# A streaming-encoder block in split float32: value groups' outputs moved to the end of a step, a projection's wait narrowed to its own bank, its pieces spread over other steps

## What is computed

```python
h = rmsnorm(x)
a_q, a_k, a_v, b_q, b_k, b_v, c_q, c_k, c_v, c_f, gates = split(h @ w_in)
# A: 4 heads, two score maps each, mask by chunks, value width 128
a = softmax(q1 @ k1.T * scale + bias) - lam * softmax(q2 @ k2.T * scale + bias)
o_a = rmsnorm(a @ a_v) * (1 - lam_init)
# B: 8 heads of 64, a band of at most 5 key tiles of 128 a query tile
o_b = softmax(b_q @ b_k.T * scale + rel_bias, over the band) @ b_v
# C: 8 heads of 64, causal, with a cumulative forget bias
o_c = softmax(c_q @ c_k.T * scale + c_i - c_j, causal) @ c_v
x = x + (sum_i sigmoid(gates_i) * (o_i @ w_br_i)) @ w_out
x = x + (silu(g) * u) @ w_down, with g, u = split(rmsnorm(x) @ w_gate_up)
out = rmsnorm(x)
```

## Time and profile before

| | |
|---|---|
| median of 3 runs | 2151.11 us (2147.57 to 2158.26) |
| the profiled execution | 2156.16 us, span 2154.3 us |
| TensorE busy | 1988.8 us, 92% of the span |
| VectorE busy | 999.7 us, 46% |
| ScalarE busy | 710.8 us, 33% |
| GpSimd busy | 94.5 us, 4% |
| mean granted TensorE clock | 0.98 |

### The profile page before, as it was taken

One profiled execution on the slowest core, in us unless ns is written; L12 is line 12 of the kernel. 1 busy time (PEld: TensorE's weight loads), 2 busy tenths in 40 slices (PEclk: granted clock), 3 DMA queues, 4 the chain that ended last, 5 costly groups with the idle time before them and its releaser, 6 DMA issues. The chain is left out here.

```text
span 2154.3 us, 26265 instructions
## 1 busy us (share of the span) xinstructions
PE 1988.8 (92%) x9542; PEld 1647.9 (76%) x9542; DVE 999.7 (46%) x1950; ACT 710.8 (33%) x1310; POOL 94.5 (4%) x59
## 2 busy tenths in 40 slices
PE   7888988888888888899999999999999999999997
PEld 3777777777777777778787887878888888888886
DVE  4355555565556556732433225754333333333326
ACT  5344444554545445522233112241111111111122
POOL 1110100100100000000000000000000000000000
PEclk9999999999999999999999999999999999999998
DMA  6412222122212211031211113102111111111111
GB/s 218 127 50 50 75 64 61 43 50 61 68 49 50 69 53 31 30 118 44 83 45 53 49 44 147 59 20 59 59 49 31 47 49 58 49 49 29 49 59 78
DMA packets 145268, 133.32 MB, mean 62 GB/s; under 512 B 7476, under 2 KB 130484, under 8 KB 142888
## 3 DMA queue, kind: packets, MB, share of 16 engines
q1 hardware_dynamic: 141768, 132.16, 20.8%
q10 hardware_dynamic: 3424, 0.17, 0.1%
HBM read 109.17 MB, written 16.06 MB: 58 GB/s over the span
## 5 line engine op out<-in xcount | busy, mean ns | idle before, releaser
L182 PE MATMUL ps<-h_hi,w_hi 128*128 128x512 f32 x1664 | 674.3, 405 | 51.2 <-DVE k_stack L745 37.4
L184 PE MATMUL ps<-h_hi,w_lo 128*128 128x512 f32 x1664 | 658.9, 396 | 0.0
L183 PE MATMUL ps<-h_lo,w_hi 128*128 128x512 f32 x1664 | 658.8, 396 | 0.0
L182 PEld LDWEIGHTS ps<-h_hi,w_hi 128*128 128x128 f32 x1664 | 318.8, 192 | 121.9 <-DVE k_stack L745 37.0
L184 PEld LDWEIGHTS ps<-h_hi,w_lo 128*128 128x128 f32 x1664 | 318.7, 192 | 69.5
L183 PEld LDWEIGHTS ps<-h_lo,w_hi 128*128 128x128 f32 x1664 | 319.6, 192 | 62.0
L1598 DVE TENSOR_TENSOR residual<-residual,ps 128x512 f32<-128x512 f32 x240 | 162.6, 685 | 113.9 <-PE ps L184 109.2
L956 PE MATMUL ps<-ident_r,probs_bc 128*128 128x128 f32 x528 | 85.2, 285 | 51.9 <-DVE probs_bc L813 36.3
L1589 DVE TENSOR_TENSOR w_lo<-w_raw,w_hi 128x1024 fp32r<-128x1024 f32 x46 | 56.4, 1226 | 158.4 <-ACT w_hi L1491 158.4
L1499 ACT ACTIVATE bias<-ps 128x512 f32<-128x512 f32 x44 | 26.1, 594 | 311.5 <-PE ps L184 311.5
L184 PE MATMUL ps<-w_down_hi,act_lo 128*128 128x512 f32 x320 | 124.5, 389 | 0.0
(11 more groups left out here) (202 smaller groups left out, 2714.9 us busy)
## 6 DMA issues: line engine op xcount, KB each, us to landing
w_raw<-in_w_in SPq DMA_DIRECT2D x60, 512.0 KB, 3.8
w_raw<-in_w_gate_up SPq DMA_DIRECT2D x44, 512.0 KB, 3.7
k_stack<-k_stack SPq DMA_DIRECT2D x24, 512.0 KB, 6.4
w_raw<-in_w_down SPq DMA_DIRECT2D x22, 512.0 KB, 3.5
x_all<-in_x SPq DMA_DIRECT2D x8, 512.0 KB, 8.7
bias<-bias_a_scratch SPq DMA_DIRECT2D x4, 1024.0 KB, 5.9
heads_bc_scratch<-heads_out SPq DMA_DIRECT2D x8, 512.0 KB, 3.1
bias<-neg_c_scratch SPq DMA_DIRECT2D x4, 1024.0 KB, 5.3
```

Source lines behind the costliest of these rows:

```text
L182: nc.tensor.matmul(out, w_hi, x_hi, start=first, stop=False)
L183: nc.tensor.matmul(out, w_hi, x_lo, start=False, stop=False)
L184: return nc.tensor.matmul(out, w_lo, x_hi, start=False, stop=last)
```

## The change

Four things change, all in attention. The outputs of value groups (`o_low_*` on ScalarE, `o_out_*` on VectorE) move from the start of an odd step to its end. For it the inverse row sums of A get eight columns instead of four, and a value group of B and C waits for the output of the group before it (`c["outs"] + g`), where it waited for the one before that. Groups 1 and 2 of a projection go to banks 6 and 1 (from 1 and 6), and a group waits for the emptying of the last group that used its own bank. The scores of step 8 wait for three emptied groups of the next unit instead of two. The tables of pieces, emptying and slabs change.

```diff
-PIECES_AT = [2, 2, 2, 2, 0, 2, 2, 0, 2, 2, 0, 1, 1, 1, 1, 0, 0]
-EVAC_AT = {0: 0, 2: 1, 4: 2, 7: 3, 10: 4, 16: 5}
-SPLIT_AT = {0: 1, 5: 2, 10: 3}
+PIECES_AT = [2, 2, 2, 2, 1, 1, 1, 1, 0, 1, 1, 1, 1, 1, 1, 2, 0]
+EVAC_AT = {0: 0, 2: 1, 4: 2, 8: 3, 13: 4, 16: 5}
+SPLIT_AT = {0: 1, 4: 2, 8: 3}
+PROJ_BANKS = (3, 6, 1, 6, 6, 6)
...
@@ ScalarE, and in the same way VectorE with o_out_a and o_out_bc
                 for s in range(STEPS + 2):
-                    if b == 0 and s >= 3 and s % 2 == 1:
-                        o_low_a(c, (s - 3) // 2)
-                    if b > 0 and s >= 3 and s % 2 == 1:
-                        o_low_bc(c, (s - 3) // 2)
...
+                    if b == 0 and s >= 3 and s % 2 == 1:
+                        o_low_a(c, (s - 3) // 2)
+                    if b > 0 and s >= 3 and s % 2 == 1:
+                        o_low_bc(c, (s - 3) // 2)
...
@@ TensorE, piece
                 if part == 0 and not (isinstance(unit, int) and unit == 0):
-                    pe.wait_ge(proj_out, 6 * unit + g)
+                    same = [x for x in range(g) if PROJ_BANKS[x] == PROJ_BANKS[g]]
+                    pe.wait_ge(proj_out, 6 * unit + (same[-1] + 1 if same else 0))
@@ TensorE, score
                 if s == STEPS // 2 and not last:
-                    pe.wait_ge(proj_out, 6 * c["unit"] + 8)
+                    pe.wait_ge(proj_out, 6 * c["unit"] + 9)
@@ TensorE, times_v_bc
-                if g >= 2:
-                    pe.wait_ge(o_out, c["outs"] + (g - 1))
-                elif b == 1 and g == 0:
-                    pe.wait_ge(o_out, c["outs"])
+                pe.wait_ge(o_out, c["outs"] + g)
```

More of the change, by code:

```diff
@@ L442, in block_attention @@
         mask_tile = heads[:, 0:P]
-        neg_max, shift, rowsum, rinv = (sb(n, [P, 4]) for n in ("neg_max", "shift", "rowsum", "rinv"))
+        neg_max, shift, rowsum = (sb(n, [P, 4]) for n in ("neg_max", "shift", "rowsum"))
+        rinv = sb("rinv", [P, 8])
         ratio = sb("ratio", [P, 2])
@@ L479, in proj_bank @@
                 return bank(ps, (0, 1, 2, 3, 5, 6)[g] if unit == 0 else 6)
-            return bank(ps, (3, 1, 6, 6, 6, 6)[g])
+            return bank(ps, PROJ_BANKS[g])
         def pv_half(g):
@@ L674, in o_low_a @@
                 nc.scalar.activation(o_low[:, i % 2 * P:(i % 2 + 1) * P], pv_bank[:, P:2 * P], ACT.Copy,
-                                     scale=rinv[:, 2 * (i % 2):2 * (i % 2) + 1]).then_inc(o_low_ready, 1)
+                                     scale=rinv[:, 2 * (i % 4):2 * (i % 4) + 1]).then_inc(o_low_ready, 1)
             def o_low_bc(c, g):
@@ L819, in mix_maps @@
                 dve.wait_ge(probs_ready, c["step"] + (2 * i + 2))
-                nc.vector.reciprocal(rinv[:, q:q + 2], rowsum[:, q:q + 2]).then_inc(rinv_ready, 1)
+                r = 2 * (i % 4)
+                nc.vector.reciprocal(rinv[:, r:r + 2], rowsum[:, q:q + 2]).then_inc(rinv_ready, 1)
                 dve.wait_ge(rinv_ready, c["outs"] + (i + 1))
-                nc.vector.tensor_scalar(ratio[:, i % 2:i % 2 + 1], rowsum[:, q:q + 1], rinv[:, q + 1:q + 2],
+                nc.vector.tensor_scalar(ratio[:, i % 2:i % 2 + 1], rowsum[:, q:q + 1], rinv[:, r + 1:r + 2],
                                         keep["neg_lam"][:, :], ALU.mult, ALU.mult).then_inc(ratio_ready, 1)
@@ L836, in o_out_a @@
                 nc.vector.scalar_tensor_tensor(out=heads[:, i * P:(i + 1) * P], in0=pv_bank[:, 0:P],
-                                               scalar=rinv[:, 2 * (i % 2):2 * (i % 2) + 1], in1=o_low[:, i % 2 * P:(i % 2 + 1) * P],
+                                               scalar=rinv[:, 2 * (i % 4):2 * (i % 4) + 1], in1=o_low[:, i % 2 * P:(i % 2 + 1) * P],
                                                op0=ALU.mult, op1=ALU.add).then_inc(o_out, 1)
@@ L864, in unit_body @@
                 for s in range(STEPS + 2):
[L865 to L868, removed]
                     if b == 0 and s % 2 == 0 and s < STEPS:
@@ L878, in unit_body @@
                         chunks_low(b, c, s)
+                    if b == 0 and s >= 3 and s % 2 == 1:
+                        o_out_a(c, (s - 3) // 2)
+                    if b > 0 and s >= 3 and s % 2 == 1:
+                        o_out_bc(c, (s - 3) // 2)
             for g in range(4):
```

## The result

The changed kernel takes 2069.27 us (median of 4 runs, 2067.87 to 2072.79) where the kernel before, timed beside it, takes 2154.69 (4 runs, 2147.57 to 2161.72). The ratio is 0.961, with a 95% interval of 0.957 to 0.964: 85 us faster. The forecast was 2064 in a range of 2030 to 2112. The profiled execution has 2067.87 us, where the prediction's sum, made against the profiled execution of before, gave 2067.

A forecast was written before the change was run, and what follows sets the result against it. Only attention can gain: TensorE's work plus 106.7 us of waits and 28 us of low clock. Waits 11 + 33 + 26 = 70 us and clock 19 give 89 off, so 2064 us, range 2030 to 2112.

The forecast's parts named there:

- Term 1: Attention's projection pieces wait only for their own bank; the k_stack waits, 37.4 us, go and nothing takes their place.
- Term 2: Pieces in steps 4 to 15 cover softmax-chain waits; B falls from 42.2 us by 33, C from 35.2 by 26.
- turn(9): In B, the turn behind the emptying of group 3 at step 8 waits 1.55 us in place of 2.44.
- Turn(10): In B, the weight slab split at step 8 holds up a scaling and delays this turn by 0.35 us.
- a scaling of 512 columns took 1.20 us ... so 0.65 more: VectorE's scaling at step 8 takes 0.65 us more while GpSimd splits a weight slab.
- the 12 us that the prediction put beside its sum by that page: If scalings stand still for GpSimd's whole 2.40 us instruction, the saving is 12 us less in seven units; not adopted.
- Term 3: Outputs at the step's end: waits for the previous output in A, about 4.5 us a unit; covered in B and C.
- In the same measure: In attention, the clock's cost of 28 us falls like the waits, by two thirds, 19 us.
- The rival by the page TensorE: Matmul & The Clock Gate of the Trainium skill: Clock stays low in attention though waits go; 2081 us, chance 0.15 of the main forecast case (itself 0.70).
- (b): Rival: only k_stack waits go, late softmax-chain waits stay as latency; 2109 us, range 2095 to 2130; chance 0.17.
- (e): Rival: slower, value groups wait for the exponential everywhere; 2177 us at 1.2 us a group; chance 0.04.
- The signs: Right if no k_stack wait, B and C units 9 to 11 us shorter, A 3 to 6, clock 0.98 or more.

The follow-up runs named there:

- The quarters: Changed kernel with GpSimd's low part of a weight slab made in four instructions of a quarter each in attention: 2065.81 us, 0.959 of the kernel before.
- the slab at step 14: Changed kernel with the last weight slab of a unit split in step 14 instead of 8: 2061.26 us, 0.958 of the kernel before.

## Why the prediction was right, and where its terms were off

**What bounds the kernel.** Right. The feed-forward block did not move, and in attention the time is TensorE's work, its waits and the clock: in the sum 60 us of waits and 26 of clock went (27 by TensorE's busy time), 86 of the 88 us between the two profiled executions. The rest is 1.1 us before and behind the eleven units, and rounding.

**Term 1.** Right: 37.4 us of k_stack waits go, and what takes their place is the 1.1 us on w_lo in A, which was not forecast; shown by the banks alone, where the waits of the softmax chain stay to 0.2 us.

**Term 2.** The mechanism was right, the term mis-sized: B keeps 15.9 us, not 9.4, C 16.3, not 9.2. That most late waits want cover, and get it from the spread pieces, is shown by the tables alone (65 to 30 us). In the second unit of B, turn(9) was forecast at 1.55 and measured at 1.80; its chain left out a link, that the turn's bank must be freed by the first low chunk behind the scaling. Turn(10) was forecast at 0.35 and measured at 1.39. In a unit of C, turn(9) has 2.09 for 1.6, turn(10) 0.96 for 0.35, and 1.13 at turn(6), which was not forecast, also behind a scaling held by GpSimd. The held scalings are most of the error: 4 x 1.04 + 3 x (0.61 + 1.13) = 9.4 of the 13.6 us by which B and C kept more. It rests on the step "a scaling of 512 columns took 1.20 us ... so 0.65 more": this is how long the scaling is held when GpSimd began 1.5 us earlier, as in the earlier trace rows, not what the meeting costs. Begun 0.27 us after it, as in the new order, a scaling of 640 columns is held 1.92 us. The earlier trace rows could have told so: the scaling there ends 0.30 us behind GpSimd's instruction. The quarters (no scaling held by more than 0.5 us) and the slab at step 14 both bring B's waits to 10.2 us, 5.7 less. The Trainium skill (SBUF — State Buffer, section "Who interferes with whom") says that the loser stands still for the other's whole instruction; the trace agrees, with 2.47 us against 0.55 where both begin together, and the 12 us that the prediction put beside its sum by that page are near these 9.4.

**Term 3.** The three waits in A are where they were put: in the first unit 0.77 us at step 8 (forecast 1.2), 1.57 at step 10 (2.0), 0.72 at step 13 (1.1), so A keeps 14.4 us instead of 18. B and C have next to no wait on heads_out (0.7 us in all), and in the kernel with the outputs alone, which has no pieces in the late steps, they have 12.4: the cover of piece, score and turn was the right reason. What failed is the view of the move in A as a price alone: against the kernel without it A gains 15 us, 7.7 of waits and 7.0 of clock, because the second score read and the emptying of group 4 come earlier.

**The clock.** Forecast 19 us back, measured 28 less 2, so 26. "In the same measure" as the waits is the step that was off: a third of 28 us should have stayed. By the other experiments there is no such measure: the outputs alone took 4 us of waits and 19 of clock away; with more waiting in A the clock rose to 1.00, with less waiting in B (15.9 to 10.2 us) it fell from 1.00 to 0.98. The rival by the page TensorE: Matmul & The Clock Gate of the Trainium skill, section "Why this matters for your kernels" (the clock stays where it was, 2081), is refuted here: every branch is at 0.99 or more after, and before it fell though no wait of these units was longer than 2.6 us.

**The sum** came out within a microsecond in the profiled execution by luck: 10 us more waits were left and 7 us more of clock came back, and the 3 between them were made up by small things outside both terms. Of the rivals, (b), only k_stack goes, is what the banks alone give (2102 for its 2109); with the pieces spread as well the late waits did go, so they were not mere latency. (e) is there in the outputs alone, at 12.4 us, too little to turn the sign.

**The signs** came in part. No wait on k_stack is left, A is 5.9 us a unit shorter (3 to 6 forecast), C 9.9 (9 to 11), and the waits on heads_out are where they were put. B is 8.4 shorter, just under the 9 forecast. The wait at turn(9) is put down to probs_tb_lo and not to probs_bc. By name, then, a sign of being wrong is there too: B has 12.0 us of waits on probs_tb_lo before and 13.9 after. But they are other waits: in the second unit of B those of 1.34 us late in the unit are gone, and the two long ones stand at the turns of rows 9 and 10.

**Open.** What decides whether the clock falls behind a wait of 1.7 to 2.2 us was not found; it fell behind some and not behind others. In the eleven units the clock falls 17 times before and once after, 1.7 us of busy time each by the difference (27.2 / 16), while the waits of 1.6 us or longer went from 38 to 8. Fewer long waits thus go with fewer falls, but no run here gives a rule, nor says why the clock gave back 26 us and not 19. Whether the outputs could stand last with the old, looser wait of the value groups was not tried; the price of the stricter wait in the changed kernel is read from its trace alone. Nor was the new order of pieces tried apart from the new steps of emptying.

## What to carry to other kernels

A wait that counts "all before" on a shared semaphore is worth narrowing to the buffer that is really reused: here it was over half the gain when made alone (54 of 85 us), and 1.1 us of it came back at another wait. In engines with a written order, put what waits longest for another engine (the output behind an exponential) at the end of the step, and what others wait for (the score read) at its start; cover the stricter wait with independent work in the same steps. When an instruction on GpSimd or VectorE is moved, ask with what on the other of the two it will now start together, and price the meeting by what is then left of the other's instruction, not by the delay seen once. And since short waits and the clock do not move in step, check a small gain in waits against TensorE's busy time too.

## What the hardware showed unexpectedly

- A scaling of 128x640 that starts 0.27 us after GpSimd's 2.39 us instruction takes 2.47 us instead of 0.55. Over the kernel 17 of 128 scalings are held, together 31.7 us, where before it was 13 and 6.6 us; each held scaling ends 0.08 to 0.36 us after GpSimd's instruction, whenever that began. With GpSimd's work in quarters they are back at the time of before, for 18 us more of GpSimd.
- The granted clock does not follow the time waited. A with 32.7 us of waits had 1.00, A with 29.3 us 0.97; B with 15.9 us had 1.00, in two profiles of the same kernel, B with 10.2 us 0.98. A microsecond taken off the waits can be lost there, so a gain of a few microseconds has to be timed, not summed.
